# Expert biases of an MoE layer: from selection products on TensorE to rows broadcast by DMA and written into PSUM by ScalarE

## The chip, the cores and the metric

The kernel runs on one core of a Trainium2 chip. The metric is the device time of one execution in microseconds. A core has TensorE (PE) for matrix products into the eight banks of PSUM, VectorE (DVE), ScalarE (ACT) and GpSimd (POOL) for element-wise work, SyncE (SP), which here issues most transfers, and 16 DMA engines.

## The reference, cut to what matters

Two transformer blocks on 512 tokens of width 1024, all in float32. The first holds a mixer, a mixture of 32 experts (four for each token) and a gated side path; the second holds attention, a recurrent group and a dense feed-forward part. The change is in the experts:

```
gu = xb @ w_gate_up[e] + b_gate_up[e]        # [rows, 1024] @ [1024, 2048] + [2048]
gate, up = split(gu, 2)
gate = minimum(gate, 7); up = clip(up, -7, 7)
act = (up + 1) * gate * sigmoid(1.702 * gate)
y = act @ w_down[e] + b_down[e]              # times the token's gate, added to its row
```

## The kernel before, in words

Tokens are sorted by expert into blocks of CAP = 96 slots, and each block belongs to one expert. With these inputs there are T = 32 blocks; the number is read at run time, and every engine runs a loop over b from 1 behind an unrolled block 0.

A block's weights are 12 pieces of 128x2048 floats (1 MB each), loaded by SP (L396) into twelve places of a ring. Pieces 0 to 3 are the first half ("chunk" 0) of the gate/up weights, 4 to 7 the second half, 8 to 11 the down weights. They are worked on in the order 0, 1, 10, 11, 2, 3, 4, 5, 6, 7, 8, 9 (ORDER), where the two pieces 10 and 11 are the rest of the block before's down product. To keep float32 accuracy each piece is split: ACT writes the rounded part (split_hi, L626), DVE the remainder (split_lo, L1448), and PE multiplies three times, high by high, high by low, low by high (L1006 to L1008). A piece is 12 products of 512 columns. SP may load a piece again when PE has counted it in the semaphore `used`; the loads of block b are thus let go one by one by PE's work on block b-1.

Banks 0 and 1 collect gate and up of chunk 0, banks 2 and 3 those of chunk 1, banks 6 and 7 the down product. Bank 4 + c takes the transposes of chunk c's activations (turn, L1014); from there ACT (L672) and DVE (L1480) split them. GpSimd gathers the next block's token rows by an indirect DMA into `xg` (L493); PE transposes them (gathered, L978) into banks 0 and 1 (6 and 7 for block 0), and ACT (gathered_hi, L632) and DVE (gathered_lo, L1473) split them; the semaphore x_lo counts the latter. ACT's sigmoid is L667, DVE's three steps behind it are L1490 to L1493, and ACT's copy of the output, times the gates, is L681.

The bias of a block, with 1 added to its up part, is put in by products: `bias_tab` holds the biases of all 32 experts (64 rows: high parts and remainders), `sel_cur` a column of zeros and ones for the block's expert repeated over the 96 slots, and PE opens each of the banks 0 to 3 with one product of the two (biases, L1022). GpSimd writes `sel_cur` for each block (select, L499). The table is loaded once (L465), has its 1 added by GpSimd (L468) and is split by ACT (L658) and DVE (L1441).

The order on each engine is the order of the code: block_pe on PE, the loop bodies on ACT and DVE, block_loads on SP, block_pool on GpSimd.

Of the kernel before, what the change touches and what calls it, by code (L numbers as in the profile page):

```python
# [19 lines left out]
ALU = mybir.AluOpType  # L20
# [7 lines left out]
P = 128  # L28
# [96 lines left out]
def build(nc, a):  # L125
    ctx = ExitStack()
    with ctx:
# [41 lines left out]
        def pcol(name, n=0):  # L169
# [41 lines left out]
        braw = v(20480, 4 * 512)  # L211
        bias_tab = vr(12288, 4 * 512)
        sel_cur = vr(7680, CAP)
        sel_all = v(7808, NB_META)
# [84 lines left out]
            idx_kept tok_kept rows_in bias_in bias_one bias_hi bias_split sel_ready hi_done lo_done used gate_done  # L299
# [50 lines left out]
        def xt_bank(b, q):  # L350

            return bank[6 + q] if isinstance(b, int) and b == 0 else bank[q]
# [9 lines left out]
        def _(sp):  # L362
# [82 lines left out]
        def _(pool):  # L445
# [18 lines left out]
            pool.wait_ge(s["hnT_ready"], KT)  # L464
            pool.dma_start(braw, a["bgu"]).then_inc(s["bias_in"], 16)  # L465
            pool.wait_ge(s["bias_in"], 16)
            up_bias = braw.rearrange("p (c h n) -> p c h n", c=CHUNKS, h=2)[0:2 * E, :, 1, :]
            pool.tensor_scalar(up_bias, up_bias, 1.0, None, ALU.add).then_inc(s["bias_one"], 1)  # L468

# [27 lines left out]
            def select(b):  # L497

                pool.tensor_copy(sel_cur, sel_all[:, bass.ds(b, 1)].broadcast_to([P, CAP])).then_inc(s["sel_ready"], 1)  # L499

# [13 lines left out]
            def block_pool(b, first):  # L514
# [10 lines left out]
                wait_counted("used", after(b, PLACE[4]))  # L525
                select(b + 1)

            gather(0)
            select(0)
# [15 lines left out]
        def _(act):  # L545
# [64 lines left out]
            def split_hi(b, s_, first=False, last=False):  # L610
# [5 lines left out]
                elif s_ == 0:  # L616
                    act.wait_ge(s["bias_split"], 1)
# [30 lines left out]
            for g in range(2 * TT):  # L648
# [7 lines left out]
                if g == 1:  # L656
                    act.wait_ge(s["bias_one"], 1)
                    act.activation(bias_tab, braw, ACT.Copy).then_inc(s["bias_hi"], 1)  # L658
# [33 lines left out]
            gathered_hi(0)  # L692
            split_hi(0, 1, True)
            for s_ in range(4, 9):
                split_hi(0, s_, True)
            first_chunk(0, True)
            with act.Fori(1, BLOCKS + 1) as b:
                with act.If(b <= T):
                    with act.If(b < T):
                        split_hi(b, 0)  # L700
                        sigmoids(b - 1, 1)
# [4 lines left out]
                        for s_ in range(3, 8):  # L706
                            split_hi(b, s_)
                        outputs(b - 1)
                        split_hi(b, 8)
                        first_chunk(b)  # L710
                    with act.If(b == T):
                        sigmoids(b - 1, 1)
                        split_hi(b, 2, last=True)
# [153 lines left out]
        def _(pe):  # L867
# [133 lines left out]
            pe.wait_ge(s["bias_split"], 1)  # L1001

# [57 lines left out]
            def block_pe(b, first):  # L1060
                pe.wait_ge(s["x_lo"], b + 1)
                pe.wait_ge(s["sel_ready"], b + 1)
                biases(0)
# [6 lines left out]
                biases(1)  # L1070
# [22 lines left out]
            pe.wait_ge(s["sel_ready"], T + 1)  # L1093
# [757 lines left out]
```

## Time and profile before

| | us |
|---|---|
| median of 3 runs | 2258.12 (2255.58 to 2258.39) |
| the profiled execution | 2256.9 |
| its span in the profile | 2255.1 |
| PE busy | 2164.3 (96%) |
| DVE busy | 1521.4 (67%) |
| ACT busy | 1073.4 (48%) |
| POOL busy | 234.9 (10%) |
| the loop over the blocks | from about 307 to 1448 |

Times in a row are microseconds from the start of the span. The matrix products overlap one another in the records, so the start of one and the start of the next tell the pace, not the duration of one. "L626" is line 626 of the kernel. In brackets behind an instruction stands how long its engine stood idle before it, and what released it. The queue of SP ("SPq") is not an engine: its wait is the time in which no load could be issued. "Landing" is the time from a transfer's issue to its completion.

### The profile page before, as it was taken

Reading aid. Unit: us, or ns where it says so; the run is one execution under the profiler, and the core shown is the slowest. Engines: PE = TensorE matmul, PEld = TensorE weight load, DVE = VectorE, ACT = ScalarE, POOL = GpSimd, SP = SyncE. Lnnn points to the kernel's source line nnn. Section 1 sums busy time; section 2 is a strip of 40 time slices with the busy share of each in tenths; the row PEclk is TensorE's granted clock in tenths of the full one; section 3 lists DMA queues with packets and bytes.
Section 4 is the critical chain, followed back from the end, with each engine's and each line's share of the span. In section 5 each row is a group of like instructions: output and inputs, shape, how many; then the busy total and the mean of one; then the engine's idle time right before and its main releaser. Section 6 shows DMA issues by size and latency. Waiting matters only on the chain.

```text
span 2255.1 us, 25922 instructions
## 1 busy us (share of the span) xinstructions
PE 2164.3 (96%) x8736; PEld 1432.9 (64%) x8736; DVE 1521.4 (67%) x1575; ACT 1073.4 (48%) x950; POOL 234.9 (10%) x239
## 2 busy tenths in 40 slices
PE   8999999999999999999999999689997899999998
PEld 3445457777777777777777777445643346888886
DVE  3953369999999999999999999544614633333333
ACT  1010147777777777777777777420002423222222
POOL 0003311112111111121211211100000000000000
PEclk9998989999999999999999999889998899999999
DMA  6123379999999999999999999611221011222220
GB/s 255 56 84 114 121 317 340 377 376 382 376 374 381 373 384 373 382 379 373 384 372 381 382 370 380 254 38 38 94 93 47 1 38 56 94 94 98 108 94 37
DMA packets 77756, 522.63 MB, mean 232 GB/s; under 512 B 10208, under 2 KB 10736, under 8 KB 21264
## 3 DMA queue, kind: packets, MB, share of 16 engines
q1 hardware_dynamic: 65088, 483.95, 55.4%
q0 software_dynamic: 9168, 31.01, 5.4%
q10 hardware_dynamic: 3456, 7.06, 1.0%
q8 instruction: 30, 0.49, 0.1%
q14 instruction: 14, 0.11, 0.0%
HBM read 500.98 MB, written 18.99 MB: 231 GB/s over the span
## 4 chain that ended last, share of the span: by engine, by line
PE 90%; DVE 7%; ACT 1%; DMA 1%; issue 1%; SPq 0%; DVEq 0%; ACTq 0%; POOLq 0%
PE bank L1006 21%; PE bank L1008 21%; PE bank L1007 21%; PE bank L872 13%; PE bank L1118 6%; DVE room L1301 3%; PE bank L1022 1%; PE bank L1133 1%; PE bank L1216 1%; PE bank L978 1%; PE bank L1014 1%; PE bank L881 1%; PE bank L1198 1%; DVE room L1640 1%; DVE room L1662 0%
## 5 line engine op out<-in xcount | busy, mean ns | idle before, releaser
L1448 DVE TENSOR_TENSOR ring_r<-ring,room_r 128x2048 fp32r<-128x2048 f32 x384 | 873.3, 2288 | 90.1 <-ACT room_r L626 87.3
L626 ACT ACTIVATE room_r<-ring 128x2048 fp32r<-128x2048 f32 x384 | 735.7, 1917 | 189.0 <-PE bank L1008 183.3
L1006 PE MATMUL bank<-room_r 128*96 128x512 f32 x1536 | 607.1, 395 | 3.5 <-DVE room_r L1480 1.9
L1008 PE MATMUL bank<-room_r 128*96 128x512 f32 x1536 | 603.1, 393 | 0.0
L1007 PE MATMUL bank<-ring_r,room_r 128*96 128x512 f32 x1536 | 603.0, 393 | 0.0
L1008 PEld LDWEIGHTS bank<-room_r 128*96 128x96 f32 x1536 | 248.8, 162 | 105.7
L1006 PEld LDWEIGHTS bank<-room_r 128*96 128x96 f32 x1536 | 248.9, 162 | 105.4 <-DVE ring_r L1448 4.4
L1007 PEld LDWEIGHTS bank<-ring_r,room_r 128*96 128x96 f32 x1536 | 249.0, 162 | 101.0 <-issue 0.2
L872 PE MATMUL bank<-ring,room 128*128 128x512 f32 x544 | 238.9, 601 | 4.0 <-ACT room L587 3.3
L872 PEld LDWEIGHTS bank<-ring,room 128*128 128x128 f32 x544 | 104.7, 194 | 134.5 <-issue 133.5
L1118 PE MATMUL bank<-room,ring 128*128 128x512 f32 x320 | 140.4, 597 | 0.0
L1006 PE MATMUL bank<-room_r,ring_r 128*128 128x512 f32 x352 | 137.2, 390 | 0.9 <-DVE room_r L1699 0.9
L1008 PE MATMUL bank<-room_r,ring_r 128*128 128x512 f32 x352 | 137.1, 389 | 0.0
L1007 PE MATMUL bank<-room_r,ring_r 128*128 128x512 f32 x352 | 137.1, 389 | 0.0
L510 POOL DMA_INDIRECT sum_rows<-room,idx_row x32 | 48.3, 1508 | 602.4 <-ACT room L681 566.3
L1118 PEld LDWEIGHTS bank<-room,ring 128*128 128x128 f32 x320 | 60.7, 192 | 72.1 <-issue 71.5
L846 ACT ACTIVATE room<-bank 128x512 f32<-128x512 f32 x22 | 13.2, 598 | 176.0 <-PE bank L1008 176.0
L872 PE MATMUL bank<-room,ring 128*128 128x512 f32 x208 | 89.8, 593 | 0.0
L1677 DVE TENSOR_TENSOR ring_r<-ring,ring_r 128x2048 fp32r<-128x2048 f32 x33 | 75.4, 2287 | 17.6 <-ACT ring_r L819 17.6
L1708 DVE TENSOR_TENSOR room<-room,bank 128x512 f32<-128x512 f32 x22 | 15.1, 687 | 91.4 <-PE bank L1008 91.4
L1006 PEld LDWEIGHTS bank<-room_r,ring_r 128*128 128x128 f32 x352 | 66.1, 188 | 14.7 <-issue 1.1
L1008 PEld LDWEIGHTS bank<-room_r,ring_r 128*128 128x128 f32 x352 | 66.1, 188 | 13.8
(243 smaller groups left out, 2053.8 us busy)
## 6 DMA issues: line engine op xcount, KB each, us to landing
ring<-in_wmoe SPq DMA_DIRECT2D x384, 1024.0 KB, 11.6
ring<-in_wf SPq DMA_DIRECT2D x33, 1024.0 KB, 4.8
ring<-in_wp SPq DMA_DIRECT2D x9, 2048.0 KB, 7.8
ring<-in_wd SPq DMA_DIRECT2D x7, 2048.0 KB, 8.9
ring<-in_wd SPq DMA_DIRECT2D x3, 1024.0 KB, 8.1
room<-in_xT SPq DMA_DIRECT2D x2, 1024.0 KB, 8.4
room<-in_xtok ACTq DMA_DIRECT2D x1, 2048.0 KB, 7.7
h_rows<-room POOLq DMA_DIRECT2D x4, 512.0 KB, 3.1
```

The lines of the kernel that those rows point to most:

```text
L510: pool.indirect_dma_start(sum_dram, bass.IndirectOffsetOnAxis(ap=idx_row[0:CAP, :], axis=0), y_sb[0:CAP, :], None, bounds_check=S + CAP - ...
L626: act.activation(w_hi[s_ % PAIRS], raw_w[ORDER[s_]], ACT.Copy)\
L872: ins = pe.matmul(out, lhsT, rhs, start=(k == 0), stop=(k == n - 1))
L881: pe.matmul(bank[j][:, :], w0[:, k, j * P:(j + 1) * P], xT[:, k, :], start=(k == 0), stop=False, skip_group_check=True)
L978: ins = pe.transpose(xt_bank(b, k // 4)[:, (k % 4) * CAP:(k % 4 + 1) * CAP], xg[0:CAP, k * P:(k + 1) * P], ident[0:CAP, 0:CAP])
L1006: pe.matmul(out, x_hi, w_hi, start=start, stop=False, skip_group_check=True)
L1007: pe.matmul(out, x_hi, w_lo, start=False, stop=False, skip_group_check=True)
L1008: return pe.matmul(out, x_lo, w_hi, start=False, stop=stop, skip_group_check=True)
L1118: ins = pe.matmul(bank[j % 2][:, :], w[:, k, c:c + P], uT[:, k, :], start=(k == 0), stop=(k == KT - 1))
L1301: step(dve.scalar_tensor_tensor(o, upad[:, i, k:k + S], w, o, ALU.mult, ALU.add))
L1448: dve.tensor_tensor(w_lo[i], raw_w[i], w_hi[s_ % PAIRS].bitcast(F32), ALU.subtract)\
L1677: dve.tensor_tensor(f_lo[f % FPAIRS], fraw_w[f % FRAW], f_hi[f % FPAIRS].bitcast(F32), ALU.subtract)\
```

## The change

The bias table in DRAM becomes one row of 2048 floats for each expert. For each block SP loads its expert's row, broadcast to 96 partitions, into `bias_rows`: for block 0 ahead of the other loads, for a later block between the loads of pieces 3 and 4, behind a wait on bias_put for the block before. ACT writes the four quarters of it into banks 0 to 3 (put_bias), the up parts with 1 added, in two pairs; each pair waits for the transfer (bias_in) and for the activations of the block before, which read the banks. PE's products then all add to what stands in the bank, and the first of a chunk waits for bias_put. The selection products, `sel_cur`, `sel_all`, the load and split of the table and their semaphores are gone.

The transposes of the gathered rows go to banks 4 and 5 instead of 0 and 1. For that PE waits for act_lo of chunk 0 ahead of them (it did so behind them), and ahead of the transposes of chunk 1 it waits for x_lo of the next block. In the last round ACT and DVE also split the rows gathered for the block behind the last.

```diff
         def xt_bank(b, q):
-            return bank[6 + q] if isinstance(b, int) and b == 0 else bank[q]
+            return bank[6 + q] if isinstance(b, int) and b == 0 else bank[4 + q]
...
             def block_loads(b, first):
                 expert = sp.value_load(meta[0:1, bass.ts(b, 1)], min_val=0, max_val=E - 1)
+                if first:
+                    sp.dma_start(bias_rows, a["bgu"][bass.ts(expert, 1)].broadcast_to([CAP, 4 * 512])).then_inc(s["bias_in"], 16)
                 for i in range(PIECES):
+                    if i == 4 and not first:
+                        sp.wait_ge(s["bias_put"], b * CHUNKS)
+                        sp.dma_start(bias_rows, a["bgu"][bass.ts(expert, 1)].broadcast_to([CAP, 4 * 512])).then_inc(s["bias_in"], 16)
...
+            def put_bias(b, c):
+                act.wait_ge(s["bias_in"], b * 16 + 16)
+                if not (isinstance(b, int) and b == 0):
+                    act.wait_ge(s["act_ready"], (b - 1) * CHUNKS + (c + 1))
+                act.activation(bank[2 * c][0:CAP, :], bias_rows[:, 2 * c * 512:(2 * c + 1) * 512], ACT.Copy)
+                act.activation(bank[2 * c + 1][0:CAP, :], bias_rows[:, (2 * c + 1) * 512:(2 * c + 2) * 512], ACT.Identity, bias=1.0)\
+                   .then_inc(s["bias_put"], 1)
...
                         split_hi(b, 0)
+                        put_bias(b, 0)
                         sigmoids(b - 1, 1)
                         gathered_hi(b)
...
                         for s_ in range(3, 8):
                             split_hi(b, s_)
+                            if s_ == 4:
+                                put_bias(b, 1)
...
             def turn(b, c):
                 pe.wait_ge(s["act_ready"], b * CHUNKS + (c + 1))
+                if c == 1:
+                    pe.wait_ge(s["x_lo"], b + 2)
...
-            def biases(c):
-                for h in range(2):
-                    q = 2 * c + h
-                    pe.matmul(bank[q][0:CAP, :], sel_cur, bias_tab[:, q * 512:(q + 1) * 512], start=True, stop=False,
-                              skip_group_check=True)
...
                 c, at = divmod(i, 4)
+                if at == 0:
+                    pe.wait_ge(s["bias_put"], b * CHUNKS + (c + 1))
...
                 gate_up(b, 9)
+                pe.wait_ge(s["act_lo"], b * CHUNKS + 1)
                 gathered(b + 1)
                 if not first:
                     pe.wait_ge(s["y_copied"], b * 2)
-                pe.wait_ge(s["act_lo"], b * CHUNKS + 1)
                 down(b, 10)
```

On ACT, the beginning of the loop's body in the kernel before (L626 splits a piece, L667 is the sigmoid of the block before, L632 copies the gathered rows, L672 the transposed activations):

```order
L615 ISA [waits raw_in0]
L626 ACTIVATE room_r<-ring0 128x2048 [waits used]
L666 ISA
L667 ACTIVATE room<-bank2 96x512 [waits gate_done]
L630 REGISTER_ALU
L632 ACTIVATE room_r<-bank0 128x4x96 [waits xt_ready]
L632 ACTIVATE room_r<-bank1 128x4x96
```

and in the changed kernel, where the same lines are L612, L650, L618:

```order
L603 ISA [waits raw_in0]
L612 ACTIVATE room_r<-ring0 128x2048 [waits used]
L671 ISA [waits bias_in]
L672 ACTIVATE bank0<-room 96x512 [waits act_ready]
L673 ACTIVATE bank1<-room 96x512
L649 REGISTER_ALU
L650 ACTIVATE room<-bank2 96x512 [waits gate_done]
L616 REGISTER_ALU
L618 ACTIVATE room_r<-bank4 128x4x96 [waits xt_ready]
L618 ACTIVATE room_r<-bank5 128x4x96
```

A wait for the DMA and two writes to PSUM now stand between the first split and the sigmoid, and the gathered rows are read from banks 4 and 5.

On SP, the loads of pieces 3 and 4 in the loop (L396) before:

```order
L396 ISA [waits used]
L396 DMA ring1<-in_wmoe 128x2048
L391 REGISTER_ALU
L396 ISA [waits used]
L396 DMA ring2<-in_wmoe 128x2048
```

and in the changed kernel (L398):

```order
L398 ISA [waits used]
L398 DMA ring1<-in_wmoe 128x2048
L390 REGISTER_ALU
L391 ISA [waits bias_put]
L391 DMA room<-in_bgu 96x2048
L393 REGISTER_ALU
L398 ISA [waits used]
```

The broadcast of the next block's bias row, with a wait of its own, has come in behind the load of piece 3.

## Rows read from the trace of the kernel before

**Rows 1.** The page's chain that ended last, by engine.
```profile
PE 90%; DVE 7%; ACT 1%; DMA 1%; issue 1%; SPq 0%; DVEq 0%; ACTq 0%; POOLq 0%
```

**Rows 2.** Waits of SP's queue, 340 to 1420 us: total, times, longest.
```profile
SPq L396 <- PE bank L1008: 795.7, 262, 8.5
```

**Rows 3.** PE: timeline of one block (start, duration), and all bias products (ns min/median/max).
```profile
307.35 1.14 PE L1022 MATMUL bank<-room_r 128*96 128x512 f32 x2 [2.27 <-DVE room_r L1473]
...
711.71 0.62 PE L1022 MATMUL bank<-room_r 128*96 128x512 f32 x2
712.17 0.39 PE L1006 MATMUL bank<-room_r 128*96 128x512 f32 x1
...
729.74 0.49 PE L1014 MATMUL bank<-cst,room 96*128 96x96 f32 x4
...
747.10 0.62 PE L1022 MATMUL bank<-room_r 128*96 128x512 f32 x2
...
L1022 PE MATMUL bank<-room_r x128: 390/392/711, 307.4 to 1419.7; 128*96 128x512 f32 x128
```

**Rows 4.** Windows: length, busy by engine (PE, PEld, DVE, ACT, POOL), PEclk, DMA share, GB/s.
```profile
500.00:700.00 200.00, 200.00 (x932) 142.38 (x931) 186.00 (x128) 150.60 (x113) 34.33 (x35) 1.00 1.00 377
716.00:718.00 2.00, 2.00 (x14) 1.43 (x12) 2.00 (x2) 1.05 (x1) 0.00 (x0) 1.00 1.03 305
722.00:724.00 2.00, 2.00 (x14) 1.50 (x13) 1.91 (x2) 1.50 (x2) 1.09 (x2) 1.00 1.03 434
1439.90:1443.00 3.10, 3.06 (x9) 2.11 (x10) 2.29 (x1) 0.46 (x1) 0.00 (x0) 0.63 0.99 423
```

**Rows 5.** SP's loads of pieces 1, 3 and 6: issue, and landing where given.
```profile
L396 SPq DMA_DIRECT2D ring<-in_wmoe x1: 332/332/332, 709.0 to 709.0; - x1
DMA to landing us min/median/max: 10.8/10.8/10.8
...
L396 SPq DMA_DIRECT2D ring<-in_wmoe x1: 333/333/333, 712.0 to 712.0; - x1
...
L396 SPq DMA_DIRECT2D ring<-in_wmoe x1: 333/333/333, 721.1 to 721.1; - x1
DMA to landing us min/median/max: 12.8/12.8/12.8
```

**Rows 6.** ACT: timeline of the same block.
```profile
720.98 1.92 ACT L626 ACTIVATE room_r<-ring 128x2048 fp32r<-128x2048 f32 x1 [0.47 <-PE bank L1008]
723.05 0.59 ACT L667 ACTIVATE room<-bank 96x512 f32<-96x512 f32 x1
724.41 0.87 ACT L632 ACTIVATE room_r<-bank 128x384 fp32r<-128x384 f32 x2 [0.76 <-PE bank L978]
```

**Rows 7.** DMA issues from 1685 to 1695: count, size, landing.
```profile
ring<-in_wp SPq DMA_DIRECT2D x1, 2048.0 KB, 7.6
rowvec<-in_rows SPq DMA_DIRECT2D x1, 512.0 KB, 8.5
```

**Rows 8.** DVE: timeline of the same block.
```profile
725.76 0.67 DVE L1492 TENSOR_TENSOR room<-bank,room 96x512 f32<-96x512 f32 x1
726.46 0.69 DVE L1493 SCALAR_TENSOR_TENSOR room<-room 96x512 f32<-96x512 f32 x1
727.07 1.01 DVE L1473 TENSOR_TENSOR room_r<-bank,room_r 128x384 fp32r<-128x384 f32 x2
728.00 4.48 DVE L1448 TENSOR_TENSOR ring_r<-ring,room_r 128x2048 fp32r<-128x2048 f32 x2
732.40 0.55 DVE L1480 TENSOR_TENSOR room_r<-bank,room_r 128x384 fp32r<-128x384 f32 x1
```

**Rows 9.** PE: timeline of the first and the last block, after waits.
```profile
316.81 0.48 PE L1006 MATMUL bank<-room_r 128*96 128x512 f32 x1 [1.63 <-DVE ring_r L1448]
...
1439.94 0.47 PE L1006 MATMUL bank<-room_r 128*96 128x512 f32 x1 [1.91 <-DVE room_r L1480]
...
1440.71 0.63 PE L1006 MATMUL bank<-room_r 128*96 128x512 f32 x1
1441.14 0.63 PE L1007 MATMUL bank<-ring_r,room_r 128*96 128x512 f32 x1
```

More of the change, by code:

```diff
@@ L209, in build @@
         plet = v(6656, S)
[L211 to L214, printed above, removed]
+        bias_rows = v(12288, 4 * 512)[0:CAP]
         xg = v(4096, D)
@@ L298, in build @@
             gm_ready gT_ready GT_ready pleg_ready plep_ready ple_parts ple_evac bdn_ready bdn_done idx_in sum_begun
-            idx_kept tok_kept rows_in bias_in bias_one bias_hi bias_split sel_ready hi_done lo_done used gate_done
+            idx_kept tok_kept rows_in bias_in bias_put hi_done lo_done used gate_done
             sig_done act_ready xt_ready x_hi x_lo turned act_hi act_lo y_copied ln2_rows_in fin_row_in c2_in v2_ready s2_ready x2_ready ss_ready
@@ L523, in block_pool @@
                 keep_rows(b)
-                wait_counted("used", after(b, PLACE[4]))
-                select(b + 1)
             gather(0)
-            select(0)
             for i in range(TT):
@@ L655, in _ @@
                     act.activation(GT[0:E, :], bank[6][0:E, :], ACT.Copy).then_inc(s["GT_ready"], 1)
-                if g == 1:
-                    act.wait_ge(s["bias_one"], 1)
-                    act.activation(bias_tab, braw, ACT.Copy).then_inc(s["bias_hi"], 1)
             act.wait_ge(s["meta_ready"], 3)
@@ L692, in _ @@
             gathered_hi(0)
+            act.wait_ge(s["bdn_done"], 2 * TT)
+            put_bias(0, 0)
             split_hi(0, 1, True)
+            put_bias(0, 1)
             for s_ in range(4, 9):
@@ L712, in _ @@
                         sigmoids(b - 1, 1)
+                        gathered_hi(b)
                         split_hi(b, 2, last=True)
@@ L999, in _ @@
             pe.wait_ge(s["bdn_done"], 2 * TT)
-            pe.wait_ge(s["bias_split"], 1)
             def product(out, x_hi, x_lo, w_hi, w_lo, start, stop):
@@ L1061, in block_pe @@
                 pe.wait_ge(s["x_lo"], b + 1)
-                pe.wait_ge(s["sel_ready"], b + 1)
-                biases(0)
                 gate_up(b, 0, first)
@@ L1069, in block_pe @@
                 gate_up(b, 5)
-                biases(1)
                 gate_up(b, 6)
@@ L1090, in _ @@
                         rest_of_down(b, True)
-            pe.wait_ge(s["sel_ready"], T + 1)
             pe.wait_ge(s["y_copied"], T * 2)
@@ L1430, in _ @@
             step(dve.tensor_scalar(metaf[:, 0:NB_META], metaf[:, 0:NB_META], float(E - 1), None, ALU.min))
-            step(dve.tensor_scalar(sel_all, metaf[:, 0:NB_META], pcol("expert"), None, ALU.is_equal))
             dve.tensor_copy(meta[0:1, 0:NB_META], metaf[0:1, 0:NB_META]).then_inc(s["meta_ready"], 1)
@@ L1437, in _ @@
             dve.tensor_copy(meta[0:1, META_T:META], end[0:1, E - 1:E]).then_inc(s["meta_ready"], 1)
-            dve.wait_ge(s["bias_hi"], 1)
-            dve.tensor_tensor(bias_tab[E:2 * E, :], braw[E:2 * E, :], bias_tab[E:2 * E, :].bitcast(F32), ALU.subtract)\
-               .then_inc(s["bias_split"], 1)
             def split_lo(b, s_, edge=False):
@@ L1521, in _ @@
                         activations(b - 1, 1)
+                        gathered_lo(b)
                         split_lo(b, 2, True)
@@ L1834 @@
     arrays["pT"] = x["p"][0, 0].reshape(S, 2, P).transpose(2, 1, 0).reshape(P, 2 * S)
-    bgu = np.zeros((P, 4 * 512), np.float32)
-    bgu[0:E] = bgu[E:2 * E] = x["b_gate_up"][0].reshape(E, 2, CHUNKS, 512).transpose(0, 2, 1, 3).reshape(E, -1)
-    arrays["bgu"] = bgu
+    arrays["bgu"] = x["b_gate_up"][0].reshape(E, 2, CHUNKS, 512).transpose(0, 2, 1, 3).reshape(E, -1)
     arrays["bdn"] = x["b_down"][0]
```

9 lines of the change are left out of this document (removed).

## The prediction

> **What bounds the kernel now.** I read the chain of work that ended last first: 90% of it is TensorE (PE) [rows 1], so elsewhere time counts only where it reaches PE. The loop over the 32 expert blocks is the half of the span from 307 to 1448 us, and inside it the list of waits has no line for PE at all; the DMA queue of SP waits for PE instead [rows 2]. In PE's own timeline one product starts every 0.23 us (two bias products from 711.71, the next at 712.17), and a block repeats after 747.10 - 711.71 = 35.39 us [rows 3]. So each PE instruction taken out of a block is worth its full pitch, as long as nothing else becomes late.
>
> Two neighbours have to be looked at before that is believed. ScalarE (ACT) is busy 151 of 200 us and VectorE 186 of 200 in the loop, and the DMA engines show a share of 1.00 at 377 GB/s [rows 4]: ACT has some 9 us a block left, and the DMA has no idle share to show, though nobody waits for it. The change takes work from the first (PE) and gives it to these two. A load that nobody is late for can still land long after it is issued: 10.8 and 12.8 us for 1 MB here [rows 5].
>
> **What is removed.** Four bias products a block, 128 in all [rows 3], at 0.23 us: 29.4 us. The first pair runs at half pace (1.14 us busy where a later pair shows 0.62) [rows 3], which adds 0.5 us: 29.9 us in all, and every block has the gain since PE is the bound. GpSimd's copy of a selector column, its load and addition on the table and the split of the table on ACT and VectorE lie ahead of or beside the loop; none is followed by a PE wait in the loop. I count them at nothing.
>
> **ACT's new work.** Two writes of 96x512 into PSUM per half of a block. The trace has no such write; its nearest row is the sigmoid of the same shape, from PSUM to SBUF, 0.59 us [rows 6]. The bounds are 0.48 (a quarter of the 1.92 us that 2048 columns take [rows 6]) and 0.59; I take 0.6 each, 1.2 us a pair, 2.4 a block. The second pair stands after the fifth weight split, some 10 us before PE needs it, and ACT's 9 idle us a block cover it: nothing. The first pair stands right at the joint of two blocks, between the first split of the new block and the sigmoid of the old block's second half. Its own 1.2 us would also be covered. What it waits for is the question.
>
> **The wait for the bias rows.** Let t = 0 be 711.71, where PE ends the fourth gate/up piece of its block and SP is let go to issue piece 3 of the next (the row shows that issue at 712.0) [rows 5]. The broadcast, 96 x 8 KB = 0.79 MB, stands right behind it on the same queue, at about t = 0.7; the wait on bias_put ahead of it is long fulfilled by then. When does it land? The queue delivers in the order of issue. Piece 1, issued at 709.0, lands at 719.8, t = 8.1 [rows 5]. Behind it come pieces 2 and 3, 1.05 MB each, and then the rows. From 722 to 724 the DMA moves 434 GB/s [rows 4]: 2.44 us a piece, 4.9 for two, 1.83 for the bias. It lands at 8.1 + 4.9 + 1.8 = 14.8. The late bound: pieces 2 to 6 took (721.1 + 12.8) - 719.8 = 14.1 us, 2.82 each [rows 5], since gathers and accumulating stores slow the loads (305 GB/s from 716 to 718) [rows 4]; then it is 8.1 + 2.75 x 2.82 = 15.9. The early bound is the rows costing nothing behind piece 3, 13.0. That 96 reads of one row are no slower than other reads is seen later: behind a 2 MB load issued at about the same time, a broadcast of 0.5 MB landed 1.1 us after it (8.5 + 0.2 against 7.6) [rows 7]. I take 14.8, because the stretch in question is the fast one.
>
> ACT comes to this wait earlier. Its split starts at 720.98 and ends at 722.90 [rows 6]; that is t = 11.2, and 10.7 in the new kernel, since the second pair of products (0.46) is gone. So ACT stands 4.1 us in each of 31 blocks, and behind the wait are queued, on ACT: the sigmoid (0.6) and the copy of the gathered rows (0.87) [rows 6]; on VectorE: the product with the sigmoid and the two steps behind it, 725.76 to 728.08, 2.3 us [rows 8], the last of which gives x_lo.
>
> **Who waits for that.** The banks for the gathered rows move from 0 and 1 to 4 and 5, so the transposes of the activations' second half now wait for x_lo too. PE is at them at 729.74, t = 18.03 [rows 3], and 17.57 without the 0.46. The chain: 14.8 + 1.2 (pair) + 0.6 (sigmoid) + 2.3 (VectorE) + 0.1 for semaphores = 19.0. PE waits 1.5 us, 31 times: 47 us. In the old order the same three steps were done at 728.08, 1.7 us ahead of PE, which is the cover that is used up. Behind the stall ACT still has two splits and the copy of the transposed half, and VectorE 4.48 and 0.55 us [rows 8], before the product pieces of the down projection can go on; I find them about 0.3 us ahead of PE, so no second stall. The other moved wait (the first half's act_lo, now ahead of the gathered transposes) is fulfilled about 3 us early: nothing. The last block's extra copies lie between steps that wait for PE: nothing.
>
> **TensorE's clock.** A stall can cost more than itself. In the last block PE stood 1.91 us before 1439.94; 0.8 us later its products start 0.43 apart instead of 0.23 for some eight products, and the granted clock of the stretch is 0.63 (part 2.4, part 1.2 GHz) [rows 4, 9]: 1.6 us lost. Before 316.81 it stood 1.63 us and products went on at pace [rows 9]. My stall of 1.5 is nearer to the second. From none to a third of the stalls may drop the clock, 0 to 16 us; I take 5 of them, 8 us.
>
> **Sum.** -29.9 + 47 + 8 = +25 us. The profiled execution took 2256.9 us (span 2255.1), the median of the runs is 2258.1; so 2282 by the one and 2283 by the other. I predict 2283.
>
> **The DMA's capacity.** A block moves 377 x 35.39 = 13.3 MB, and 14.1 with the bias. At 434 GB/s that is 32.6 us, at 377 it is 37.5 [rows 4]; the block I forecast, 35.39 - 0.92 + 1.5 = 36.0 us, lies between. The Trainium skill ("DMA: Bandwidth & Descriptors", Bandwidth) puts the ceiling of the ports at 435 GB/s, which the trace reaches, and a limit of about 358 for reads from HBM by one core, which the measured 377 already exceeds, so the trace decides. By the skill's 435 the DMA would carry the new load with 2 us to spare; by its 358 even the kernel before could not run as it does.
>
> **Rivals.** (a) The bias lands in time. Then PE stays the bound, and the whole 29.9 us come: 2228. It needs a landing before t = 13.3; each 0.1 us later costs 3.1 us, and the point of no change is 14.2 (a stall of 0.96 us), 0.6 us ahead of my value. For it: the other loads might be further ahead when PE's own stalls give the DMA time. Against it: piece 3 alone lands near 13.0. Between 13.3 and 14.2 the time is 2228 to 2258. (b) The DMA becomes the bound: the block is 37.5 us, +2.1 x 31 = +65, 2323. For it, the share of 1.00; against it, the 434 GB/s of two microseconds within that same share of 1.00 [rows 4]. (c) The clock falls after nearly every stall: 31 x 1.6 = 50 instead of 8, 2325. For it, the row at 1439.94; against it, the one at 316.81. (d) The forecast with the landing anywhere from 14.4 to 15.9: stalls of 1.1 to 2.6 us, 2227 + 31 s, so 2261 to 2308 before the clock's share.
>
> **Chances.** Forecast (d) 0.55, (b) 0.12, (c) 0.08, (a) with all that is faster 0.19, a landing so near 14.2 that nothing is seen 0.06. About 0.2% is what a measurement of this kernel can tell from no change; that makes faster 0.19, same 0.06, slower 0.75. The range goes from 2243 (a stall of half a microsecond) to 2322 (the late landing with some loss of clock): it leaves out the full gain below, and half of (b) and (c) above.
>
> **What would show it.** Right: ACT's writes to PSUM wait some 4 us each for the DMA of the bias rows, 120 us or so in all; PE's transposes of the second half wait 1 to 2 us for VectorE's x_lo, 31 times; the block's period is about 36 us; the granted clock has dips in some blocks. Wrong: no PE wait in the loop and a period of 34.5 us (a); PE waits at weight splits that wait for loads, the period 37 us or more (b); a mean clock well below 1 in the loop (c). If the writes themselves took over 1 us, my price from the sigmoid's row would be the wrong step.

## The result and the profile after

The changed kernel takes 2420.98 us, median of runs from 2417.6 to 2422.98, beside 2258.06 for the kernel before: a ratio of 1.0722, 95% interval 1.0706 to 1.0738. The prediction was 2283 us with a range up to 2322. It had the sign right and missed the size by 138 us: 163 us were lost instead of 25, and the forecast's own upper end is 99 us short. Where the runs of one kernel below scatter by more than 1.5%, as in e2, the ratio given is that of its faster runs alone, and the median is that of all.

The chain that ended last, on the page of the changed kernel, by engine. Before, it was PE for 90% [rows 1]; now a fifth of it is DMA, nearly all of that the bias load (19% by line).

```profile
PE 65%; DMA 20%; DVE 9%; issue 3%; ACT 3%; SPq 1%; ACTq 0%; DVEq 0%; POOLq 0%
```

The waits of the changed kernel from 340 to 1600 us (total, times, longest): those of ScalarE (ACT), VectorE (DVE), TensorE (PE) and SP's queue. L672 is the first of the new writes into PSUM, L1013 the transposes, L1458 the step that gives x_lo, L650 the sigmoid, L1477 VectorE's product with it, L398 the weight loads, L1003 to L1005 the three products of a piece. PE had no line here before; SP's queue waited 795.7 us for PE [rows 2].

```profile
ACT bank L672 <- DMA room<-in_bgu: 179.2, 30, 8.9
DVE room L1477 <- ACT room L650: 141.3, 30, 7.6
...
PE bank L1013 <- DVE room_r L1458: 91.1, 30, 6.0
PE bank L1003 <- issue: 13.5, 31, 0.8
...
SPq L398 <- PE bank L1005: 976.5, 272, 17.0
```

One joint of two blocks on ACT and DVE (start, duration), answering [rows 6, 8]: the writes wait for the load, everything queued behind them on ACT waits with them, and DVE waits for the sigmoid.

```profile
695.62 1.92 ACT L612 ACTIVATE room_r<-ring 128x2048 fp32r<-128x2048 f32 x1 [0.47 <-PE bank L1005]
702.53 0.60 ACT L672 ACTIVATE bank<-room 96x512 f32<-96x512 f32 x1 [5.00 <-DMA room<-in_bgu]
703.07 0.58 ACT L673 ACTIVATE bank<-room 96x512 f32<-96x512 f32 x1
703.59 0.58 ACT L650 ACTIVATE room<-bank 96x512 f32<-96x512 f32 x1
...
743.50 0.60 ACT L672 ACTIVATE bank<-room 96x512 f32<-96x512 f32 x1 [5.57 <-DMA room<-in_bgu]
```
```profile
704.20 0.69 DVE L1477 TENSOR_TENSOR room<-bank,room 96x512 f32<-96x512 f32 x1 [3.74 <-ACT room L650]
704.92 0.69 DVE L1478 SCALAR_TENSOR_TENSOR room<-room 96x512 f32<-96x512 f32 x1
705.53 1.01 DVE L1458 TENSOR_TENSOR room_r<-bank,room_r 128x384 fp32r<-128x384 f32 x2
```

PE at the same joint, answering [rows 3]. Look at the distance of the starts: 0.23 us before the stall (684.04, 684.27), 0.43 behind it.

```profile
684.04 0.39 PE L1003 MATMUL bank<-room_r 128*96 128x512 f32 x1
684.27 0.39 PE L1004 MATMUL bank<-ring_r,room_r 128*96 128x512 f32 x1
...
706.60 0.77 PE L1013 MATMUL bank<-cst,room 96*128 96x96 f32 x4 [2.07 <-DVE room_r L1458]
707.93 0.73 PE L1003 MATMUL bank<-room_r 128*96 128x512 f32 x1 [0.56 <-issue]
708.46 0.63 PE L1004 MATMUL bank<-ring_r,room_r 128*96 128x512 f32 x1
708.89 0.63 PE L1005 MATMUL bank<-room_r 128*96 128x512 f32 x1
```

Windows of the changed kernel (length, busy by PE, PEld, DVE, ACT, POOL, then granted clock, DMA share, GB/s), answering [rows 4]: the stretch behind that stall, then most of the loop.

```profile
708.00:714.00 6.00, 6.00 (x15) 3.97 (x16) 5.92 (x4) 3.30 (x4) 0.00 (x0) 0.53 1.01 406
500.00:1300.00 800.00, 733.39 (x3110) 509.12 (x3111) 639.45 (x430) 556.08 (x472) 131.58 (x95) 0.91 0.95 346
```

The new loads (L391: count, durations of their issue, first and last start): one block in (1547.8 - 322.8) / 30 = 40.83 us, where it was 35.39 [rows 3].

```profile
L391 SPq DMA_DIRECT2D room<-in_bgu x31: 332/333/344, 322.8 to 1547.8; - x31
```

So the loss can be read on PE in two parts. Idle, 66.6 of 800 us, which is 3.4 us a block. And the clock: behind this stall the granted clock is that of 1.2 GHz for 6.8 us (706.8 to 713.6), and between 340 and 1560 us there are 29 such stretches, all but one of 6.8 us. A stretch at half speed loses half of its length, 3.4 us a block. 35.39 less the 0.92 of the products plus 3.4 plus 3.4 is 41.3, against 40.83 measured; a little is counted twice, since PE also stands for 0.56 us inside the slow stretch. That says where PE lost the time, not what started it. The DMA now moves 346 GB/s where it moved 378, though it has more to carry. In this kernel that doesn't say which is the cause: a longer block by itself lowers the rate, the DMA share is 0.95, and no engine waits for a weight piece. The experiments with the kernel before settle it, since nobody waits for their load.

### The profile page after: what moved, and what is told of

Its sections match the earlier page's. It is cut to its first block, busy times and chain, and to the rows that moved or that the text cites. A ratio compares the mean times of both kernels' runs of the same rounds, so it can differ in the third digit from the quotient of the medians.

```text
span 2420.9 us, 25796 instructions
## 1 busy us (share of the span) xinstructions
PE 2226.7 (92%) x8608; PEld 1457.6 (60%) x8608; DVE 1519.4 (63%) x1575; ACT 1124.6 (46%) x1079; POOL 262.8 (11%) x204
## 4 chain that ended last, share of the span: by engine, by line
PE 65%; DMA 20%; DVE 9%; issue 3%; ACT 3%; SPq 1%; ACTq 0%; DVEq 0%; POOLq 0%
DMA room<-in_bgu 19%; PE bank L1003 14%; PE bank L1004 14%; PE bank L1005 14%; PE bank L871 12%; PE bank L1108 6%; DVE room L1291 3%; DVE room_r L1458 1%; PE bank L1123 1%; PE bank L1013 1%; PE bank L1206 1%; DVE room L1477 1%; ACT bank L673 1%; PE bank L1188 1%; PE bank L880 1%
## 5 line engine op out<-in xcount | busy, mean ns | idle before, releaser
L612 ACT ACTIVATE room_r<-ring 128x2048 fp32r<-128x2048 f32 x384 | 731.1, 1913 | 175.5 <-PE bank L1005 172.5
L1003 PE MATMUL bank<-room_r 128*96 128x512 f32 x1536 | 639.3, 416 | 19.3 <-issue 13.5
L1004 PE MATMUL bank<-ring_r,room_r 128*96 128x512 f32 x1536 | 629.7, 410 | 0.0
L1005 PE MATMUL bank<-room_r 128*96 128x512 f32 x1536 | 628.1, 409 | 0.0
L1003 PEld LDWEIGHTS bank<-room_r 128*96 128x96 f32 x1536 | 263.0, 171 | 138.6 <-issue 27.7
L1005 PEld LDWEIGHTS bank<-room_r 128*96 128x96 f32 x1536 | 261.8, 170 | 116.0 <-issue 1.1
L1004 PEld LDWEIGHTS bank<-ring_r,room_r 128*96 128x96 f32 x1536 | 263.3, 171 | 107.7 <-issue 0.6
L1108 PE MATMUL bank<-room,ring 128*128 128x512 f32 x320 | 140.3, 596 | 0.0
L1003 PE MATMUL bank<-room_r,ring_r 128*128 128x512 f32 x352 | 137.0, 389 | 0.9 <-DVE room_r L1685 0.9
L1005 PE MATMUL bank<-room_r,ring_r 128*128 128x512 f32 x352 | 136.9, 389 | 0.0
L1477 DVE TENSOR_TENSOR room<-bank,room 96x512 f32<-96x512 f32 x64 | 43.6, 682 | 141.3 <-ACT room L650 141.3
L1013 PE MATMUL bank<-cst,room 96*128 96x96 f32 x256 | 43.1, 305 | 91.1 <-DVE room_r L1458 91.1
L672 ACT ACTIVATE bank<-room 96x512 f32<-96x512 f32 x64 | 37.6, 588 | 191.9 <-DMA room<-in_bgu 180.8
L1013 PEld LDWEIGHTS bank<-cst,room 96*128 96x128 f32 x256 | 32.7, 173 | 110.8 <-DVE room_r L1458 104.9
L495 POOL COPY idx_row<-places 96x1 uint32 (+1 forms) x32 | 67.6, 2112 | 259.9 <-DMA sum_rows<-room,idx_row 259.9
## 6 DMA issues: line engine op xcount, KB each, us to landing
ring<-in_wmoe SPq DMA_DIRECT2D x384, 1024.0 KB, 15.7
```

What stands on the lines that cost most here:

```text
L495: pool.tensor_copy(idx_row[0:CAP, :], places[0:CAP, bass.ds(b, 1), 0]).then_inc(s["idx_kept"], 1)
L612: act.activation(w_hi[s_ % PAIRS], raw_w[ORDER[s_]], ACT.Copy)\
L1003: pe.matmul(out, x_hi, w_hi, start=start, stop=False, skip_group_check=True)
L1004: pe.matmul(out, x_hi, w_lo, start=False, stop=False, skip_group_check=True)
L1005: return pe.matmul(out, x_lo, w_hi, start=False, stop=stop, skip_group_check=True)
L1013: ins = pe.transpose(bank[4 + c][:, r * CAP:(r + 1) * CAP], act_sb[c][0:CAP, r * P:(r + 1) * P], ident[0:CAP, 0:CAP])
```

## The experiments

The expectations name their theories by letters. **A**: the transfer of the rows costs, because it lands late and ACT, VectorE and PE stand behind it, with the clock's fall; from e5 on, A also says that it was the broadcast's way of reading that was slow. **B**: the new order itself costs (the writes to PSUM, the banks 4 and 5, the waits for x_lo and act_lo). **C**: the DMA traffic alone makes the loss. **D**: the bytes alone count. **E**: the shape, that is, which partitions the load writes. The ratios are against the kernel before on the same chip (2255.9 to 2257.6 us).

### The new order without the traffic

e1_rows_once leaves the later loads out, so that every block adds the first expert's bias and the output is not the right one:
```
-                    if i == 4 and not first:
-                        sp.wait_ge(s["bias_put"], b * CHUNKS)
-                        sp.dma_start(bias_rows, a["bgu"][bass.ts(expert, 1)].broadcast_to([CAP, 4 * 512])).then_inc(s["bias_in"], 16)
...
-                act.wait_ge(s["bias_in"], b * 16 + 16)
+                act.wait_ge(s["bias_in"], 16)
```


> The changed kernel with the bias rows loaded for block 0 alone: the loads of the later blocks are left out, so every block gets the first expert's bias. Theory A (what costs is the transfer of the rows: it lands late and ACT, VectorE and PE stand behind it; the clock then falls): no wait is left, the block is 35.39 - 0.92 = 34.5 us and the time 2257 - 30 = 2227 us. Rival B (the new order itself costs: the writes to PSUM, the banks 4 and 5, the waits for x_lo and act_lo): PE's waits ahead of the transposes stay, and the time is above 2258.

Measured: 2226.89 us, ratio 0.9868 [0.9852, 0.9884]. Its windows:
```profile
500.00:1300.00 800.00, 800.00 (x3715) 568.22 (x3714) 752.65 (x511) 662.36 (x558) 164.45 (x117) 1.00 1.01 388
```
PE is busy all of the time at a clock of 1.00. The removed products are worth 29.0 us (29.9 were predicted), and the new writes, the new order of ACT and the moved banks cost nothing. B is out: all of the loss comes with the load.

### The traffic without the new order

e2_before_plus_load is the kernel before, with the same load into a spare buffer:
```
+                    if i == 4 and not first:
...
+                        sp.dma_start(spare, a["bgu"][bass.ts(expert, 1)].broadcast_to([CAP, 4 * 512])).then_inc(s["start_in"], 16)
```


> The kernel before, with the broadcast of the next block's bias row to 96 partitions added at the place where the change has it; nobody reads it. Theory A: PE waits for nothing new as long as the DMA keeps up; in the changed kernel the packets of the broadcast took 0.56 us instead of 0.31, so it costs the DMA 3.1 us a block. By the landings before the change the DMA works 33 to 34 us of each 35.4, so it would need 36 to 37: up to +1.5 us a block, 2258 to 2305. Rival C (the DMA traffic alone makes the loss): near 2420.

Measured: 2349.71 us, from 2297 to 2382; ratio 1.0251 [1.0168, 1.0334]. The windows and waits of one execution (one of the upper ones; L632 is the weight split, L1020 the transposes):
```profile
500.00:1300.00 800.00, 735.36 (x3257) 513.85 (x3256) 647.27 (x438) 521.50 (x398) 102.47 (x120) 0.96 1.00 354
```
```profile
ACT room_r L632 <- DMA ring<-in_wmoe: 206.4, 75, 9.6
```
Nobody waits for this load, and yet the kernel is slower, by 57 us in the ratio, by 94 in the median of all runs and by 41 in the fastest of them: the weight pieces come late, and ACT waits for them. The rate has fallen to 354 GB/s at a DMA share of 1.00. The time lies between A's 2305 and C's 2420, so the traffic alone makes a part of the loss.

e7_before_plus_plain_load is the same with 96 rows of weights, 8 KB each, in place of one row read 96 times:
```
+                        sp.dma_start(spare, a["wmoe"][bass.ts(expert, 1), 0].rearrange("o p n -> (o p) n")[0:CAP, :]).then_inc(s["start_in"], 16)
```


> The kernel before with a load of the same size as the broadcast (96 rows of 8 KB, of the weights, each read once) at the same place, unused. Theory A: 1.8 us more for the DMA in a block of 35.4 that it filled to 34 or so: 2256 to 2275, against 2350 with the broadcast. Theory D: 2350 as with the broadcast.

Measured: 2370.55 us, ratio 1.0492 [1.0451, 1.0532], at 351 GB/s:
```profile
500.00:1300.00 800.00, 735.25 (x3252) 512.79 (x3251) 644.83 (x438) 521.43 (x398) 98.53 (x120) 0.96 1.02 351
```
An ordinary load is no cheaper. In the changed kernel it is the same: e5_table_same_place keeps a table in which each bias row stands 96 times, and reads it without a broadcast.
```
-                        sp.dma_start(bias_rows, a["bgu"][bass.ts(expert, 1)].broadcast_to([CAP, 4 * 512])).then_inc(s["bias_in"], 16)
+                        sp.dma_start(bias_rows, a["bgu"][bass.ts(expert, 1)].rearrange("o p n -> (o p) n")).then_inc(s["bias_in"], 16)
```


> The changed kernel with the table in DRAM holding each expert's bias 96 times, so that the load of 0.79 MB reads 96 rows of their own instead of one row 96 times; its place is the same. Theory A (two costs of the DMA: the broadcast's packets of 0.56 us, and its megabytes in a queue without room): the load takes 1.8 us of the DMA instead of 3.1, lands 1.3 us earlier, PE's stall goes from 3 to 1.7 us, and the DMA needs about 2 us a block less than in the changed kernel: 2290 to 2350. Theory D (the bytes alone count, not how they are read): unchanged, near 2420.

Measured: 2418.5 us, ratio 1.0714 [1.0697, 1.0732], the same as the changed kernel. That one row is read 96 times is not the cause, and A's forecast for it, 2290 to 2350, has failed.

### The place of the load, the order of ACT, and the clock

e3_row_early issues the load with the block's first piece (`i == 4` becomes `i == 0`):

> The changed kernel with the broadcast issued ahead of piece 0 instead of between pieces 3 and 4. Theory A: four pieces less stand ahead of it, it lands some 10 us earlier, before ACT comes to it, and ACT's wait for it is gone; what is left is the DMA's own load: the block between 34.5 (2227 us, if it keeps up) and 37 us (2305), with the granted clock near 1. Rival B: PE's waits ahead of the second transposes stay, 2400 or so.

Measured: 2328.36 us, ratio 1.0297 [1.0237, 1.0357]. The wait for the bias is gone, 93 us come back, and 101 us above e1 stay: ACT waits 108 us for weights (27 times) and the rate is 367 GB/s. That is above A's 2305 and below B's 2400. e6_table_early, the table read early, gave 2321 us, from 2281 to 2341: too scattered to be told from e3.

> As the run before, and the load issued ahead of piece 0. Theory A: no wait for the bias is left, and what is left of the DMA is 0.79 MB at full rate, 1.8 us a block: against 34.5 us of PE and a DMA that worked through the block's other 13.3 MB in 34.5 us without the load (rows loaded once), 36.3 us: about 2290. If that DMA still had room at 34.5, down to 2227. Theory D: as the early broadcast, 2328.

e8_put_behind_gathered leaves the load where it is and lets ACT copy the gathered rows ahead of the wait:
```
-                        put_bias(b, 0)
...
                         gathered_hi(b)
+                        put_bias(b, 0)
```


> The changed kernel with ACT's first pair of writes behind the sigmoid and the copy of the gathered rows instead of ahead of them; the broadcast as in the change. If the loss is what is queued behind ACT's wait (sigmoid, gathered rows, VectorE, x_lo): PE now waits for the writes alone, which end 1.2 us after the landing, at 17.5 us of the block, where PE arrives at 17.6; the stall goes, and about 3 us a block with it, 2330 or less. If the DMA is the bound, it gains little: above 2350, with the waits moved to the loads of the weights.

Measured: 2369.87 us, ratio 1.0492 [1.0463, 1.0521]. The wait has moved to the first product of the block, as the waits from 340 to 1600 us show:
```profile
PE bank L1003 <- ACT bank L673: 87.1, 30, 5.5
```
It takes nearly as long as the 91.1 us in the changed kernel, but the clock (0.96 instead of 0.91) falls less, and 51 us come back. The run was forecast to gain the whole stall (2330 or less) or to wait for weights instead (above 2350); the time is that of the second, but no engine waits for weights.

e4_fillers keeps TensorE at work through the stall, with six products that nobody reads:
```
+                    for _ in range(6):
+                        pe.matmul(bank[7][CAP:P, 0:2 * P], cst[:, 0:P - CAP], cst[:, P:3 * P], start=True, stop=True, skip_group_check=True)
```


> The changed kernel with six float32 products (2.6 us of PE, into rows of bank 7 that nobody reads) ahead of PE's wait for x_lo, so that PE works through most of its stall. Theory A says that of the 5.6 us a block over the kernel before, 3.4 are the clock at 1.2 GHz for 6.8 us behind each stall: with the fillers the clock stays at 2.4 GHz, the block takes 37.5 us and the time is about 2315. If the fall of the clock has nothing to do with the stall, it stays at 2420 and the clock at 0.93.

Measured: 2399.66 us, ratio 1.0611 [1.057, 1.0652].
```profile
500.00:1300.00 800.00, 766.25 (x3413) 522.76 (x3414) 649.75 (x436) 562.63 (x475) 137.29 (x99) 0.97 0.98 351
```
The clock rises from 0.91 to 0.97 (0.915 to 0.970), which is worth some 2.3 us a block, 70 in all. Only 21 us arrive, and ACT's wait for the bias grows from 179 to 202 us. At 351 GB/s the DMA doesn't deliver much faster: most of what the clock gave back went into waiting for the bias rows. The clock's fall is real and mostly a consequence. (The fillers, 2.6 us, are nearly as long as the mean stall of 3.0 us; what they themselves hold up was not told apart.)

### The shape of the load

Which leaves: why do the DMA engines move 351 to 354 GB/s in e2 and e7, at a share of 1.00 and more, when they moved 388 in e1? The trace's records of the single packets (8 KB, one row each) show it: the median of all such packets is 309 ns in the kernel before, and in the changed kernel it is 532 ns for the 94 of them that start between 698.5 and 701.5 us, just ahead of the write that waits for the bias load. (The expectations below take 560.) The Trainium skill ("SBUF — State Buffer", Door 1: The DMA port swizzle) says that partitions 0 to 63 hang on eight of sixteen ports and 64 to 127 on the other eight, with partitions 32 apart inside such a half on the same port. By that, 96 partitions put twice as much on the first eight ports as on the others, and the weight pieces, with 128, load all alike. It is a rule that can be tried.

e9_before_plus_128 adds a load into all 128 partitions, a third more bytes than e2:
```
-        spare = v(16384, 4 * 512)[0:CAP]
+        spare = v(16384, 4 * 512)
...
-                        sp.dma_start(spare, a["bgu"][bass.ts(expert, 1)].broadcast_to([CAP, 4 * 512])).then_inc(s["start_in"], 16)
+                        sp.dma_start(spare, a["bgu"][bass.ts(expert, 1)].broadcast_to([P, 4 * 512])).then_inc(s["start_in"], 16)
```


> The kernel before, with a load of one bias row broadcast into all 128 partitions (1.05 MB) added to each block from the second at the place where the change puts its load; nobody reads what it brings, and its last landing is waited for at the end. Theory D, bytes alone: the transfers of a block (12.58 MB of weights and the gathers) had the engines at a 1.00 share for 35.4 us; 1.05 MB more at the same 377 GB/s is 2.8 us a block against 2.1 us for 96 partitions, and whatever a 96-partition load costs, this one costs a third more: the 96-partition load gave 2349.7 us beside 2257, so 2375 us or more here. Theory E, the shape: in the 96-partition loads a packet of 8 KB takes 560 ns instead of 309 because the partitions are unevenly spread over whatever the engines share on the SBUF side; a load of 128 partitions has the shape of the weight pieces, its packets take 309 ns, and the block grows by no more than 1.05 MB at 434 GB/s = 2.4 us, less what slack there is: 2257 to 2332 us, below the 96-partition load in spite of more bytes. (The Trainium skill, page SBUF - State Buffer, section Door 1: The DMA port swizzle, gives partitions 0 to 63 eight of the sixteen ports and 64 to 127 the other eight, by which 96 partitions put twice the load on the first eight; it is the reason to ask, and enters no number here.)

Measured: 2268.29 us, ratio 1.0047 [1.0031, 1.0064].
```profile
500.00:1300.00 800.00, 793.96 (x3668) 562.26 (x3667) 723.61 (x492) 587.63 (x445) 104.71 (x135) 1.00 1.02 401
```
More bytes, and 11 us lost, where 96 partitions cost 57 (e2, by the ratio) to 114 (e7). The engines now move 401 GB/s; the 377 of the kernel before was no ceiling. D, the theory of bytes, has fallen. Then the sharpest pair: the same 64 rows, 0.52 MB, put into partitions 0 to 63 (e12_64_rows_at_0) or into 32 to 95 (e13_64_rows_at_32).
```
-        spare = v(16384, 4 * 512)[0:64]
+        spare = v(16384, 4 * 512)[32:96]
```


> The kernel before, with a bias row broadcast into partitions 0 to 63 (0.52 MB) added to each block from the second, at the change's place, unused. Theory E, which partitions are written: the packets of such a load take 560 ns as those of the 96-partition load did, 0.52 MB then goes at 234 GB/s, 2.2 us a block, where 128 partitions cost 0.4 us a block beyond the kernel before: 2290 us or more. Theory G, that a load has not 128 rows: the same as e13, 2290 us or more in both. Theory H, 96 rows as such (six packets on each engine): below the 128-partition load in both, 2257 to 2268 us. (The Trainium skill, page SBUF - State Buffer, section Door 1: The DMA port swizzle, puts these 64 partitions on eight of sixteen ports; by it alone this load is dear and that of e13 is cheap.)

> As e12, with the same 64 rows written into partitions 32 to 95: the same bytes, packets and place, other partitions alone. Theory E: 2257 to 2270 us, at least 20 us below e12. Theory G: as e12, 2290 us or more. Theory H: as e12, 2257 to 2268 us.

Measured: 2348.49 us, ratio 1.0386 [1.0344, 1.0428], against 2257.48 us, ratio 0.9998 [0.9989, 1.0008]. The windows of e12, and the DMA issues from 500 to 1300 us (size, median from issue to landing):
```profile
500.00:1300.00 800.00, 759.46 (x3401) 532.04 (x3400) 674.00 (x458) 545.54 (x417) 94.24 (x126) 0.97 1.01 361
```
```profile
ring<-in_wmoe SPq DMA_DIRECT2D x250, 1024.0 KB, 23.6
```
And those of e13:
```profile
500.00:1300.00 800.00, 800.00 (x3712) 568.24 (x3711) 740.27 (x502) 603.49 (x452) 114.99 (x138) 1.00 1.01 392
```
```profile
ring<-in_wmoe SPq DMA_DIRECT2D x271, 1024.0 KB, 12.9
```
The same bytes, packets, issue and place cost 91 us in one set of partitions and nothing in the other. By the Trainium skill's table of ports the first set puts eight rows on each of eight ports and none on the others, the second four rows on each of the sixteen; the runs agree with that, and theories G and H are out. The weight pieces land after 23.6 us in e12 (median) and after 12.9 in e13.

Two windows show it closely. The first is the slowest stretch of its block in e12, where the load was issued at 692.9 (its landing is not in the trace); the second is the last 6 us before the load of e13, issued at 677.7, landed at 691.3:
```profile
708.00:714.00 6.00, 2.49 (x13) 1.43 (x11) 5.31 (x7) 5.56 (x7) 0.00 (x0) 1.00 1.01 208
```
```profile
685.00:691.00 6.00, 6.00 (x33) 4.39 (x32) 5.72 (x5) 4.62 (x6) 3.23 (x4) 1.00 1.02 430
```
The records of the 8 KB packets between 500 and 1300 us say that weight pieces are slowed with it: 128 packets a block take over 500 ns in e12, and at most 64 of them can be the load's own. In e2 it is 163 a block, in the kernel before 45, in e13 15 and in e9 less than one. Note the DMA share: 1.01 at 361 GB/s and 1.01 at 392. It tells that packets are under way, not how fast they go.

### The shape and the place in the changed kernel

e14_128_same_place is the changed kernel with 128 partitions filled instead of 96, e10_128_early the same with the load at the block's first piece:
```
-        bias_rows = v(12288, 4 * 512)[0:CAP]
+        bias_rows = v(12288, 4 * 512)
...
-                        sp.dma_start(bias_rows, a["bgu"][bass.ts(expert, 1)].broadcast_to([CAP, 4 * 512])).then_inc(s["bias_in"], 16)
+                        sp.dma_start(bias_rows, a["bgu"][bass.ts(expert, 1)].broadcast_to([P, 4 * 512])).then_inc(s["bias_in"], 16)
```


> The changed kernel with the bias row broadcast into 128 partitions instead of 96, at the place where the change has it, ahead of the fifth piece of the block. What it differs in from the changed kernel is the shape; from the run with 128 partitions early (2269.1 us) the place. If the place costs what the prediction said of it, a stall of 1.5 us in each of 31 blocks: 2269 to 2316 us, ScalarE waiting some 4 us a block for the load. If nearly all of the loss is the shape: under 2300 us. If the shape mattered for the early load alone: 2380 us or more.

> The changed kernel, with the bias row broadcast into 128 partitions instead of 96 and issued with the first weight piece of the block (as in the run with the row early, 2328.4 us, where 96 partitions were filled). Theory D, bytes alone: slower than 2328, about 2350 us. Theory E, the shape: 2228 + 31 x 0 to 2.4 us = 2228 to 2302 us. In both no engine waits for the bias load.

Measured: e14 2349.3 us, ratio 1.0414 [1.0395, 1.0433]; e10 2269.05 us, ratio 1.0054 [1.0038, 1.0071]. Windows of e14 and its waits from 340 to 1600 us:
```profile
500.00:1300.00 800.00, 748.52 (x3337) 522.30 (x3335) 676.69 (x457) 588.38 (x501) 147.30 (x105) 0.97 0.98 375
```
```profile
ACT bank L672 <- DMA room<-in_bgu: 139.7, 30, 5.6
...
PE bank L1013 <- DVE room_r L1458: 51.6, 30, 2.7
PE bank L1003 <- issue: 22.5, 31, 0.8
```
And the windows of e10, where the rows are there before anybody asks:
```profile
500.00:1300.00 800.00, 775.98 (x3557) 543.63 (x3556) 721.14 (x492) 627.06 (x532) 99.42 (x112) 1.00 1.02 400
```
e14 lies in none of its three ranges: neither the place nor the shape is nearly all. The 194 us between e1 (2227) and the changed kernel (2421) divide: 72 us are the shape (2421 to 2349), 80 us are the place in the queue with ACT's wait behind it (2349 to 2269), 42 us are what the bytes of a whole 128-partition load cost even then. The parts depend on the order in which they are taken: with the load early, the shape costs 59 us (2328 to 2269; the runs of e3 go from 2314 to 2346). The last 42 us are the DMA as the bound: e9 and e10 end at 2268 and 2269 us with 401 and 400 GB/s, though PE has 29 us less to do in e10, and ACT waits for weights in both (62 and 73 us). The place costs more than the 47 us that the prediction gave it, since the clock comes on top of 51.6 us of stalls: 0.97, 24 us in 800.

### No wide transfer at all

e11_gpsimd_spread loads the single row of 8 KB on GpSimd's queue behind the gather of the block and lets GpSimd copy it into the 96 partitions:
```
+            def spread(b):
+                wait_counted("bias_in", b * 16 + 16)
+                wait_counted("bias_put", b * CHUNKS)
+                pool.partition_broadcast(bias_rows, bias_row, channels=CAP).then_inc(s["bias_spread"], 1)
...
-                act.wait_ge(s["bias_in"], b * 16 + 16)
+                act.wait_ge(s["bias_spread"], b + 1)
```


> The changed kernel without the wide transfer: GpSimd loads the one row of 8 KB of the next block's expert (a single descriptor's worth of data) and copies it into 96 partitions itself with a partition broadcast, behind the gather of the next block's rows; ScalarE waits for that copy where it waited for the load. If the loss of the change is the 0.79 MB of DMA a block and nothing else, this gives what the run with the later loads left out gave, 2227 us, plus whatever GpSimd's copy delays: the gather ahead of it and the copy lie before ScalarE's first write of the block after, some 25 us later. Theory A, DMA alone: 2222 to 2235 us, faster than both kernels. Rival F: the copy on GpSimd takes more than 10 us or slows VectorE by the port that they share: 2240 us or more.

Measured: 2229.77 us, ratio 0.9886 [0.9869, 0.9902], computing all of what the kernel before computes. GpSimd's timeline in one block, and the windows:
```profile
616.60 0.54 POOL L491 DMA_DIRECT2D room<-in_bgu  x1 [0.20 <-issue]
625.48 3.28 POOL L496 PARTITION_BROADCAST room<-room  x1 [8.34 <-ACT bank L688]
```
```profile
500.00:1300.00 800.00, 800.00 (x3715) 568.20 (x3714) 780.74 (x513) 661.37 (x557) 249.70 (x162) 1.00 1.01 388
```
The copy takes 3.3 us on an engine that was busy a sixth of the time, VectorE is busy for 4% longer than in e1 with nearly the same instructions (511 in 752.65 us, 513 in 780.74), and PE stays busy all of the time. Of the 29 us that the idea of the change is worth, 27 arrive (2229.77 against 2256.95); its transfer was the trouble. This version is faster than both kernels.

## Why the prediction was wrong, point by point

**The removed products: right.** 29.9 us predicted, 29.0 in e1.

**ACT's writes: right.** 0.6 us each; the group of L672 on the page has a mean of 588 ns for 64. The second pair, the moved banks and act_lo cost nothing, as e1 shows.

**The landing of the bias rows: the step that failed.** It was put at t = 14.8, which is 14.1 us behind the issue at 0.7, with t = 15.9 as its late bound. In the changed kernel, between 500 and 1300 us, L672 starts 15.7 us behind the issue of its load in the mean, which is t = 16.4: 1.6 us late, and beyond the late bound. The term that was too small is the load's own, 1.8 us at the rate of the weight pieces. The step "96 reads of one row are no slower than other reads" was true of the reading (e5) and missed the writing: it was argued from rows of a load with another shape [rows 7], and the 434 GB/s of the fast stretch [rows 4] were those of 128-partition pieces. With 128 partitions at the same place (e14) the same measure is 14.5 in spite of a third more bytes, for which the forecast's own sum would give 14.7. (In that sum 1.05 MB at 434 GB/s is 2.42 us, not 2.44, which moves nothing.)

**The DMA's capacity: right rows, wrong use.** The prediction bounded it by 377 and 434 GB/s, and took the added load to go at the rate of the others. With loads of even shape the engines do reach 401; with this one, where nobody waits for it, they fall to 354 (e2), below the lower bound. Rival (b), the DMA as the bound at 37.5 us a block, got 0.12, and its price was taken from the bytes alone. Its sign, a wait for weight pieces, is not in the changed kernel, where the bias rows are waited for first; it lies right under that wait and shows as soon as the load comes early (e3, 108 us). e2, where nobody waits for the load, has (1513.5 - 323.3) / 30 = 39.7 us a block in its profiled run.

**The stall: right in kind, half in size.** ACT waits for the bias, the sigmoid and VectorE's steps come behind it, PE waits at the transposes: each link is in the rows above. ACT's wait is 6.0 us instead of 4.1, PE's 3.0 instead of 1.5, and another 0.45 us of idle time stands ahead of the first product, for which the profile names no releaser. The 1.6 us by which the rows land late are the 1.5 us by which the stall is longer. With the even shape PE's stall is 1.7 us (e14), close to the forecast's 1.5.

**The clock: mis-sized.** 8 us were put in, from "none to a third of the stalls". The clock falls to 1.2 GHz behind nearly every stall (29 of 30), and stays there for 6.8 us, not for the eight products of [rows 9]: some 97 us at PE in place of 8. Rival (c) had the right frequency at 1.6 us a stall, where 6.8 us at half speed lose 3.4. Of the two rows it had to choose from, the one at 1439.94 was the better guide. e4 shows, however, that little of this time would have been won without it.

**The sum.** On PE the terms became -29 for the products, 105 in place of 47 for the stalls (3.4 us of idle time in 31 blocks) and 97 in place of 8 for the clock. That makes 173, with a part counted in both of the last two, where 163 were lost.

**What stays open.** That the set of partitions decides is shown, by e12 and e13. By what mechanism, is not. A count of bytes per port isn't enough: by the Trainium skill's table the 64 rows of e12 and the 128 of e9 put the same 64 KB on each of the first eight ports, and they cost 91 and 11 us. Packets of nearly twice the usual time would fit two DMA engines that meet at one port, but that is argued from the durations alone (532 and 309 ns), and the records don't say which engine carried a packet. Why packets of the weight pieces are slow beside the bad load is open too. The gathers write 96 partitions too, in both kernels; what they cost was not tried.

## What to carry to other kernels

Before a transfer is added to a stream that keeps the DMA busy, look at which partitions it writes as well as at how many bytes it has: fill all 128, or a set such as 32 to 95, rather than the first 64 or 96, or keep it small and spread it on an engine that is idle. In this change only the last was faster than the kernel before; the set 32 to 95 was tried only with a load that nobody reads. A DMA share of 1.00 says neither that there is room nor that there is none; the GB/s beside it do, compared with a run that moves more. And a new wait in the joint of two loop turns should be priced with the clock's fall behind it, then checked against what bounds the loop, since the two overlap.

## What the runs showed of the hardware that was not expected

- The same 0.52 MB a block cost nothing in partitions 32 to 95 (392 GB/s) and 91 us in partitions 0 to 63 (361 GB/s). This case's rates for one core: 378 before, 388 in e1, 401 with a 128-partition load more.
- Where the DMA is loaded so, a filled share hides a wide span of rates: 1.00 to 1.02 stood beside 351 and beside 401 GB/s.
- The clock's low stretches came once a block, 6.8 us each but for one, behind PE's stall of 3.0 us in the mean; with six filler products in the stall the mean rose from 0.91 to 0.97.
- With a load into partitions 0 to 63, packets of other transfers slowed down too: 128 a block took over 500 ns, against 45 without the load, which has 64 itself.
- GpSimd's partition broadcast of 8 KB into 96 partitions took 3.3 us; VectorE's busy time was 4% longer in that run.
